# A hybrid decoder layer with 32 experts: what moves between HBM and SBUF per expert job, where a result row is stored, and which engines split the weights and combine the results

## The reference, cut to what matters

```python
top_v, top_e = lax.top_k(logits, TOP_K)          # TOP_K = 4, N_EXPERTS = 32
top_w = jax.nn.softmax(top_v, axis=-1)
...
def expert_block(args):                          # a block: up to 128 rows of one expert
    xb, e = args
    gu = xb @ w_gate_up[e] + b_gate_up[e]
    gate = jnp.minimum(gu[:, 0::2], SWIGLU_LIMIT)
    up = jnp.clip(gu[:, 1::2], -SWIGLU_LIMIT, SWIGLU_LIMIT)
    act = (up + 1.0) * gate * jax.nn.sigmoid(SWIGLU_ALPHA * gate)
    return act @ w_down[e] + b_down[e]
...
out = jnp.zeros((T, D)).at[row_tok].add(ys * row_w[:, None])
x = x + gate2 * out
```

## Time and profile before

| | |
|---|---|
| median of 3 executions | 2153.21 us (2151.19 to 2153.41) |
| the profiled execution's own time | 2149.9 us |
| its span | 2148.1 us |
| instructions | 28297 |
| busy: PE, DVE, ACT, POOL | 89%, 74%, 52%, 41% |
| bytes moved by DMA | 534.79 MB, 249 GB/s over the span |

### The profile page before, as it was taken

The page is one execution under the profiler, slowest core; times in us unless marked ns, Lnnn a source line. Parts: engine busy times, 40 slices in busy tenths (PEclk is TensorE's granted clock), DMA queues, the critical chain, the costliest instruction groups (busy, mean ns, idle before and its releaser), DMA issues.

```text
span 2148.1 us, 28297 instructions
## 1 busy us (share of the span) xinstructions
...
## 2 busy tenths in 40 slices
...
GB/s 349 292 63 0 313 2 2 1 141 1 2 48 148 79 52 128 350 353 351 350 360 347 352 348 354 359 345 354 355 351 360 348 353 357 347 354 346 351 363 231
DMA packets 249704, 534.79 MB, mean 249 GB/s; under 512 B 10635, under 2 KB 12744, under 8 KB 248436
## 3 DMA queue, kind: packets, MB, share of 16 engines
...
HBM read 495.76 MB, written 38.29 MB: 249 GB/s over the span
## 4 chain that ended last, share of the span: by engine, by line
PE 36%; DVE 11%; issue 11%; ACT 1%; DMA 1%; DVEq 1%; POOL 1%; POOLq 0%; ACTq 0%
PE bank L1815 11%; PE bank L1816 11%; PE bank L1814 11%; DVE sb_e_lo L1770 7%; PE bank L1811 2%; PE bank L1801 1%; PE bank L1829 1%; DVE sb_x_lo L2014 1%; DVE bank L2105 1%; DVE sb_mod L2024 1%; DVE sb_a_lo L2058 1%; ACT sb_x_hi L1894 0%; DMA sb_x_slot<-h_rows,sb_row_of 0%; DVE sb_bias_pick L2010 0%; POOL sb_e_lo L1770 0%
## 5 line engine op out<-in xcount | busy, mean ns | idle before, releaser
L1770 POOL TENSOR_TENSOR sb_e_lo<-sb_w_raw,sb_e_hi 128x512 fp32r<-128x512 f32 x388 | 673.9, 1746 | 496.7 <-ACT sb_e_hi L1891 377.4
L1770 DVE TENSOR_TENSOR sb_e_lo<-sb_w_raw,sb_e_hi 128x1536 fp32r<-128x1536 f32 x388 | 810.3, 2115 | 2.2 <-ACT sb_e_hi L1891 2.2
L1891 ACT CAST sb_e_hi<-sb_w_raw 128x2048 fp32r<-128x2048 f32 x389 | 741.4, 1906 | 99.0 <-PE bank L1816 48.5
L1814 PE MATMUL bank<-sb_e_hi,sb_x_hi 128*128 128x512 f32 x1032 | 415.2, 402 | 0.0
L1816 PE MATMUL bank<-sb_e_hi,sb_x_lo 128*128 128x512 f32 x1032 | 411.1, 398 | 0.0
L1815 PE MATMUL bank<-sb_e_lo,sb_x_hi 128*128 128x512 f32 x1032 | 411.1, 398 | 0.0
L1816 PEld LDWEIGHTS bank<-sb_e_hi,sb_x_lo 128*128 128x128 f32 x1032 | 197.8, 192 | 43.8
L2027 DVE SCALAR_TENSOR_TENSOR sb_mod<-sb_mod 128x256 f32<-128x256 f32 x129 | 223.6, 1734 | 4.5
L1815 PEld LDWEIGHTS bank<-sb_e_lo,sb_x_hi 128*128 128x128 f32 x1032 | 197.7, 192 | 41.3
L1814 PEld LDWEIGHTS bank<-sb_e_hi,sb_x_hi 128*128 128x128 f32 x1032 | 198.3, 192 | 37.8
L1814 PE MATMUL bank<-sb_e_hi,sb_a_hi 128*128 128x512 f32 x512 | 208.6, 407 | 7.6 <-POOL sb_e_lo L1770 7.6
(11 more groups left out here) (380 smaller groups left out, 2773.6 us busy)
## 6 DMA issues: line engine op xcount, KB each, us to landing
...
sb_w_raw<-in_w_down_dram SPq DMA_DIRECT2D x128, 1024.0 KB, 7.3
...
```

The costliest lines, as they stand in the source:

```text
L1770: return eng.tensor_tensor(g.e_lo[:, p % PARTS, rows, :], raw(p)[:, rows, :], g.e_hi[:, p % PARTS, rows, :].bitcast(F32), ALU.subtract)
L1814: te.matmul(out, hi[:, k0 + k, :], w_hi, start=(first and k == 0 and what >= 2 * GU), stop=False)
L1891: return sc.copy(g.e_hi[:, p % PARTS, :, :], raw(p))
```

## The change

- **Rows.** The routing table now carries goals: `goal_of` holds token * 4 + k for a used slot and 4096 (`EMPTY`) for an unused one, and `row_of` is that shifted right by 2. Gathers and stores are both indirect DMAs of POOL with a bounds check, so that unused slots move nothing. The store of `g.y` goes to row token * 4 + k of `y_rows`. DVE copies the job's column of `goal_of` to `goal_now` once the former store has landed (`y_out`), inside the loop after `row`. ACT no longer issues a store. The stores that filled the unused rows of `y_rows` in the RWKV phase are gone.
- **Split.** DVE takes all four rows of a piece (128x2048). POOL takes none; its turn is a one-element operation (`tick`), the store, another `tick`, and the gather.
- **First gather.** It is issued in the routing block, as soon as `row_of` is there; `x_slot` is zeroed before.
- **The end.** The four rows of a token now lie side by side, so SP reads them back with 8 plain DMAs of 1024 KB (128 tokens, two rows each). DVE builds 12 diagonal matrices of routing weights (`diag`, 128x128) at the end of routing; PE adds three of four rows of each token with them, 24 matmuls of 128x512 f32 behind the 8 of the bias; DVE adds the fourth out of PSUM into SBUF, and multiplies and adds as before, with one 128x1024 operation each.

```diff
+EMPTY = 2 * SEQ * TOP_K
 RING = 3
 MIN_JOBS, MAX_JOBS = SEQ * TOP_K // P, (SEQ * TOP_K + N_EXP * (P - 1)) // P
-SPARE = (MAX_JOBS + 1 - MIN_JOBS) // 4
...
-    step(pool.iota(g.token[:, :], [[P, NT]], base=0, channel_multiplier=1, allow_small_or_imprecise_dtypes=True))
+    step(pool.iota(g.goal[:, :, :], [[TOP_K * P, NT], [1, TOP_K]], base=-EMPTY, channel_multiplier=TOP_K, allow_small_or_imprecise_dtypes=True))
...
-        @block.sync
-        def _(sp):
-            for i in range(SPARE):
-                at = MIN_JOBS * P + 4 * P * i
-                sp.dma_start(g.y_rows[at:at + 4 * P, :].rearrange("(p r) n -> p (r n)", r=4), g.hT[:, :, :].rearrange("p k n -> p (k n)")).then_inc(g.y_spare, 16)
...
+PE_BACK = 3
...
+def gather_rows(g, po, at):
+    po.indirect_dma_start(out=g.x_slot[:, :], out_offset=None, in_=g.h2_rows[:, :], in_offset=bass.IndirectOffsetOnAxis(ap=at, axis=0),
+                          bounds_check=SEQ - 1, oob_is_err=False).then_inc(g.x_in, 16)
+def scatter_rows(g, po, sem):
+    po.indirect_dma_start(out=g.y_rows[:, :], out_offset=bass.IndirectOffsetOnAxis(ap=g.goal_now[:, 0:1], axis=0), in_=g.y[:, :], in_offset=None,
+                          bounds_check=SEQ * TOP_K + P - 1, oob_is_err=False).then_inc(sem, 16)
...
+            po.wait_ge(*pool.at("job_of"))
+            po.memset(g.x_slot[:, :], 0.0).then_inc(*pool("x_slot"))
+            po.wait_ge(*pool.at("x_slot"))
+            po.iota(g.goal_now[:, :], [[1, 1]], base=SEQ * TOP_K, channel_multiplier=1).then_inc(*pool("spare"))
+            po.wait_ge(*pool.at("spare"))
+            po.wait_ge(g.h2_out, 16 * NT)
+            po.wait_ge(*vec.at("tok"))
+            gather_rows(g, po, g.row_of[:, 0:1])
...
-            ve.tensor_scalar(g.place_i[:, :], g.place_i[:, :], P, None, ALU.add).then_inc(*vec("at"))
...
-            of_tile = lambda x: x.rearrange("p (t k) j -> p t (k j)", t=NT)
-            ve.tensor_tensor(of_tile(g.in_job[:, :, :]), of_tile(in_job), g.token[:, :].unsqueeze(2).broadcast_to([P, NT, TOP_K * JOBS]), ALU.mult).then_inc(*vec("in_tok"))
+            goal = g.goal[:, :, :].rearrange("p t k -> p (t k)")
+            ve.tensor_tensor(g.in_job[:, :, :], in_job, goal.unsqueeze(2).broadcast_to([P, units, JOBS]), ALU.mult).then_inc(*vec("in_tok"))
...
-            ve.tensor_copy(g.row_of[:, :], ps[0][:, 0:JOBS]).then_inc(*vec("tok"))
+            then(ve.tensor_scalar(g.goal_of[:, :], ps[0][:, 0:JOBS], float(EMPTY), None, ALU.add), "goal")
+            ve.tensor_scalar(g.row_of[:, :], g.goal_of[:, :], 2, None, ALU.logical_shift_right).then_inc(*vec("tok"))
...
+            for t in ts:
+                for k in range(PE_BACK):
+                    ve.tensor_scalar(g.diag[:, t, k, :], g.ident[:, :], g.prob[:, t, k:k + 1], None, ALU.mult).then_inc(*vec(f"d{t}{k}"))
...
-        def lo_part(eng, p, rows):
-            return eng.tensor_tensor(g.e_lo[:, p % PARTS, rows, :], raw(p)[:, rows, :], g.e_hi[:, p % PARTS, rows, :].bitcast(F32), ALU.subtract)
-        def back(u):
-            part = (g.e_hi, g.e_lo)[u // (2 * PARTS)][:, u // 2 % PARTS, :, :].rearrange("p k n -> p (k n)")
-            return part[:, D * (u % 2):D * (u % 2) + D].bitcast(F32)
+            return split_done[p % PARTS], 3 * turn + 1
+        def back(t, k):
+            part = (g.e_hi, g.e_lo)[t // 2][:, 2 * (t % 2) + k // 2, :, :].rearrange("p k n -> p (k n)")
+            return part[:, D * (k % 2):D * (k % 2) + D].bitcast(F32)
+        def back_pair(t, h):
+            return (g.e_hi, g.e_lo)[t // 2][:, 2 * (t % 2) + h, :, :].rearrange("p k n -> p (k n)").bitcast(F32)
...
+            sp.wait_ge(all_stored, 1)
+            by_token = g.y_rows[0:SEQ * TOP_K, :].rearrange("(t p k) n -> t p (k n)", p=P, k=TOP_K)
+            for t in ts:
+                for h in range(2):
+                    sp.dma_start(back_pair(t, h), by_token[t][:, 2 * D * h:2 * D * h + 2 * D]).then_inc(back_in[t][h], 16)
...
-            for i in range(8):
-                t, n = i // 2, i % 2
-                te.matmul(ps[i][:, :], g.wT[:, P * t:P * t + P], g.b_down[:, 512 * n:512 * n + 512], start=True, stop=True).then_inc(*last_pe(f"b{i}"))
+            for t in ts:
+                for n in range(2):
+                    te.matmul(ps[2 * t + n][:, :], g.wT[:, P * t:P * t + P], g.b_down[:, 512 * n:512 * n + 512], start=True, stop=False)
+            for t in ts:
+                for k in range(PE_BACK):
+                    if k % 2 == 0:
+                        te.wait_ge(back_in[t][k // 2], 16)
+                    for n in range(2):
+                        mm = te.matmul(ps[2 * t + n][:, :], g.diag[:, t, k, :], back(t, k)[:, 512 * n:512 * n + 512], start=False, stop=(k == PE_BACK - 1))
+                mm.then_inc(*last_pe(f"t{t}"))
...
-                sc.wait_ge(*act.at("y1", turn))
-                sc.dma_start(g.y_rows[bass.ds(turn * P, P), :], g.y[:, :]).then_inc(y_out, 16)
...
-            def gather_rows(at):
-                return po.indirect_dma_start(out=g.x_slot[:, :], out_offset=None, in_=g.h2_rows[:, :], in_offset=bass.IndirectOffsetOnAxis(ap=at, axis=0))
+            def tick(i):
+                po.tensor_tensor(g.tick[:, i:i + 1], g.ones[:, 0:1], g.ones[:, 0:1], ALU.mult).then_inc(ticked, 1)
             jobs = job_count(po)
-            gather_rows(g.row_of[:, 0:1]).then_inc(x_in, 16)
-            for i, p in enumerate(FIRST):
-                po.wait_ge(*first_act.at(f"g{i}"))
-                lo_part(po, p, slice(VEC_ROWS, 4)).then_inc(split_done[p % PARTS], 1)
             po.wait_ge(*first_pe.at("xt1"))
-            gather_rows(g.row_of[:, 1:2]).then_inc(x_in, 16)
-            for p in range(2):
-                po.wait_ge(*first_act.at(f"h{p}"))
-                lo_part(po, p, slice(VEC_ROWS, 4)).then_inc(split_done[p % PARTS], 1)
+            gather_rows(g, po, g.row_of[:, 1:2])
             with po.Fori(0, jobs) as turn:
-                for p in list(range(2, N_POS)) + [0, 1]:
-                    po.wait_ge(*(act.before("h2", turn) if p == 2 else act.at(f"h{p}", turn)))
-                    if p == 10:
-                        po.wait_ge(row_ready, turn + 1)
-                    lo_part(po, p, slice(VEC_ROWS, 4)).then_inc(split_done[p % PARTS], 1)
-                    if p == 10:
-                        gather_rows(g.row[:, 0:1]).then_inc(x_in, 16)
-            po.wait_ge(all_stored, 1)
-            for u in range(NT * TOP_K):
-                po.indirect_dma_start(out=back(u), out_offset=None, in_=g.y_rows[:, :],
-                                      in_offset=bass.IndirectOffsetOnAxis(ap=g.place_i[:, u:u + 1], axis=0)).then_inc(back_in[u], 16)
+                po.wait_ge(*act.at("y1", turn))
+                po.wait_ge(*vec.before("goal", turn))
+                po.wait_ge(ticked, 2 * turn + 1)
+                tick(0)
+                scatter_rows(g, po, y_out)
+                po.wait_ge(row_ready, turn + 1)
+                tick(1)
+                gather_rows(g, po, g.row[:, 0:1])
+            po.wait_ge(*last_act.at("y1"))
+            po.wait_ge(last_goal, 1)
+            scatter_rows(g, po, y_out)
...
-                return lo_part(ve, p, slice(0, VEC_ROWS)).then_inc(split_done[p % PARTS], 1)
+                return ve.tensor_tensor(g.e_lo[:, p % PARTS, :, :], raw(p), g.e_hi[:, p % PARTS, :, :].bitcast(F32), ALU.subtract).then_inc(split_done[p % PARTS], 1)
...
+                ve.wait_ge(y_out, 16 * turn + 16)
+                ve.tensor_scalar(g.goal_now[:, :], g.goal_of[:, bass.ds(turn, 1)], 0, None, ALU.add).then_inc(*vec("goal"))
...
+            ve.memset(g.unused[:, 1:2], 0.0).then_inc(last_goal, 1)
             ve.wait_ge(y_out, 16 * jobs + 16)
-            for p in range(2):
-                ve.wait_ge(*is_split(p, jobs))
             ve.memset(g.unused[:, 0:1], 0.0).then_inc(all_stored, 1)
             for t in ts:
-                ve.wait_ge(*last_pe.at(f"b{2 * t + 1}"))
-                sums = [ps[2 * t + n][:, :] for n in range(2)]
-                for k in range(TOP_K):
-                    u = TOP_K * t + k
-                    ve.wait_ge(back_in[u], 16)
-                    if k:
-                        ve.wait_ge(*last_vec.at(f"k{t}{k - 1}"))
+                ve.wait_ge(*last_pe.at(f"t{t}"))
+                for k in range(PE_BACK, TOP_K):
+                    if k == PE_BACK:
+                        ve.wait_ge(back_in[t][k // 2], 16)
                     for n in range(2):
-                        mm = ve.scalar_tensor_tensor(sums[n], back(u)[:, 512 * n:512 * n + 512], g.prob[:, t, k:k + 1], sums[n], ALU.mult, ALU.add)
-                    mm.then_inc(*last_vec(f"k{t}{k}"))
-                ve.wait_ge(*last_vec.at(f"k{t}{TOP_K - 1}"))
-                for n in range(2):
-                    mm = ve.tensor_tensor(g.mod[:, t % 3, 512 * n:512 * n + 512], sums[n], g.mod[:, 3, 512 * n:512 * n + 512], ALU.mult)
-                mm.then_inc(*last_vec(f"gate{t}"))
+                        at = slice(512 * n, 512 * n + 512)
```

(12 more changed lines are left out.)

41 lines of the change are left out of this document (20 added, 21 removed).

## The result

The changed kernel takes **2047.85 us**, median of 4 runs (2047.55 to 2048.57), against 2152.2 for the kernel before beside it: ratio 0.9521, 95% interval 0.9502 to 0.954. The profiled execution took 2048.57 with a span of 2046.5 (before: 2148.1), a gain of 101.6 us in span.

A forecast was written before the change was run, and what follows sets the result against it. PE, at 38.56 us a turn, was taken to wait for DVE's splits, which POOL's splits held up. Loop -83, start -5.5 and end -5 sum to -93.5: 2149.9 to 2056.4, plus 3.3 gives 2060 us, range 2044 to 2092.

The forecast's parts named there:

- Loop, -83: Job loop: with the split on DVE alone PE never waits and keeps its clock, 38.56 to 35.97 us a turn, 32 turns.
- the turn of 35.97: Job loop: PE's turn at full clock without its wait, 36.9 less 0.93 us, taken as the new turn.
- DVE's turn, 34.6 as an upper bound: Job loop: DVE's work a turn, 12 splits of 2.3 us plus 6.5 and 0.5, below PE's 35.97.
- Routing and first gather, -5.5: Ahead of the loop: earlier gather lets PE turn rows at 852.4, not 856.9 (-4.5), plus -1; bounds 0 and -8 us.
- 12 diagonals of 0.16 us delay the next block by 1.9 us, to 850.4: End of routing: DVE's diagonals set the next block's start; PE then does a 2 us bias product and turns rows at 852.4.
- -1: Start of the loop: 1 us gained because POOL's splits and second gather are no longer ahead of the first turn.
- The end, -5: After PE's last job matmul: store landing, reads, PE's products and last tile take 41.2 us against 46.3.
- Rows, 0: Job loop: moving only used rows earns nothing by itself, since a turn's transfers, 33.8 us at 388 GB/s, stay below PE.
- The store on POOL, 0: Job loop: the store lands some 10 us into a turn, DVE's wait comes at 24 to 25; 15 us of slack, price 0.
- The end at half clock: Rival, 0.13: the end's 24 PE products don't lift the clock, 48 passes take 41 us; 19 us worse, 2079.
- Slower by the new wait: Rival, 0.03: DVE's wait for the store's landing decides, from some 27 us into a turn; landing at 40 us costs +330.
- Bounds check saves nothing: Rival, 0.04: all 128 descriptors still move, 13.6 MB a turn takes 35.1 us, still hidden; 2062 us.

The follow-up runs named there:

- e1: Kernel before, with DVE splitting all four rows and a one-element POOL operation ahead of the gather; all rows still move, ACT still stores: 2056.5 us, ratio 0.9555.
- e2: Changed kernel with POOL's quarter of each split put back, DVE doing three quarters: 2165.67 us, ratio 1.0067 to the kernel before.
- e8: Changed kernel plus 12 two-input POOL subtractions of 128x512 a turn whose result nobody uses: 2284.46 us, ratio 1.0617 to the kernel before.
- e4: Changed kernel with the twelve diagonals built by ACT during routing, not by DVE: 2046.56 us, ratio 0.9511 to the kernel before.
- e11: Changed kernel with the routing block closed without GpSimd's drain: 2042.48 us, ratio 0.9495 to the kernel before.
- e5: Changed kernel with the down-bias products 128 rows high instead of 32, zeros below row 32: 2045.13 us, ratio 0.9489 to the kernel before.
- e9: Changed kernel plus, 12 times a turn on POOL, a one-element multiplication and a one-input 128x512 operation, both unused: 2279.8 us, ratio 1.0585 to the kernel before.

## Why the prediction was right, and where it was not

The direction, the mechanism and the range (2044 to 2092) hold; 2060 was 12 us too high. Of that, 8.1 is the sum (-93.5 forecast, -101.6 by span) and 3.8 the way from span to median: I added the 3.3 by which the median of before stood above its profiled execution, and the median after stands 0.7 below its own; 0.3 goes the other way, as this execution's own time is 2.1 above its span and the one of before 1.8. The last 0.3 is rounding.

- **Loop, -83: undersized by 11.8 us.** That DVE is freed from POOL, PE stops waiting and the clock stays at 1.00 is shown by e1, e2 and e8. The failed term is the turn of 35.97, which I took as 36.9 less the idle 0.93. That idle time counts from the modelled end of the overlapped matmul before. From start to start, the step into the waiting matmul is 1.31 us in place of 0.23, so the wait cost 1.08, and 1100.01 to 1136.87 without it is 35.78. Another 0.10 is the step behind that matmul, 0.33 (1100.01 to 1100.34) where it is 0.23 in the change. The last 0.08 to 35.60 was not traced.
- **DVE's turn, 34.6 as an upper bound:** busy 1047.90 / 32 = 32.7. The split was 2.28 (forecast 2.3), L2042 0.43 as forecast.
- **Routing and first gather, -5.5: -1.2 by stage, -2.2 counted from `row_of`.** The failed step is "12 diagonals of 0.16 us delay the next block by 1.9 us, to 850.4". The diagonals took 2.42 us, but the block came at 853.4, held by POOL's drain until the gather had landed, and not by DVE (e4, e11). With the drain gone, the rows come 9.2 us after `row_of` against 14.2 before: -5.0, where I had -4.5. The "-1" for POOL's splits ahead of the first turn is there in e1 (9.9 us from the rows to the loop, 11.0 before), but not in the change (11.1): eleven passes behind the rows ran at 0.63 us there, the lower clock, against six in e1. With the bias product at full height none did, and it was 9.4 (e5). The other 1.0 of the stage is that `row_of` itself came later in this execution.
- **The end, -5: -5.6.** The store had landed by 2010.47, 4.7 us after the last job matmul (forecast 5.1), and PE ended at 33.7 (34.2). The bias products were done 10.6 us after that matmul (12.0). Half clock reached into the first 24 of the 48 passes (12.8 us, the second 24 took 10.5): 2.4 us where I had 1.7.
- **Rows, 0:** e1 moves all rows and has the same turn within 0.06 us.
- **The store on POOL, 0:** issued at 905.4, landed 7.4 us later in the median, and DVE asked for it at 927.8: 15 us of slack, as forecast. But e2, with the store beside splits on POOL, is 0.7% dearer than the kernel before, a price that I had not put down. And `tick`, put at 0.1 us, takes POOL 2.13; POOL waits long before both, so it costs nothing here.

I cited the Trainium skill (DMA: Bandwidth & Descriptors, SWDGE vs HWDGE vs iDMA) for POOL's DMAs being held off by DVE. In the change the gather took POOL 2.67 us and the store 1.01, 2.35 in e2: held off in part, and never on the path. The store at 905.38, with DVE idle or on PSUM, took 1.02; the gather at 930.61, begun inside a split, took 2.92. That rule is about DVE's two-port modes, and no run here tells whether a split runs in one. The Trainium skill, SBUF — State Buffer (Who interferes with whom), says that a Vector instruction with two SBUF inputs contends with a GpSimd instruction that reads SBUF, and that one with at most one SBUF input, outside the two-port modes, does not. The rows agree: L2042 moves between 0.43, 1.11 and 1.18, L2074 stays at 0.42. By its words e9's POOL work, which reads SBUF, contends too; measured, DVE's split took 2.34 against 2.28 us, and the loser was POOL.

**The rivals.** The end at half clock came in part: 0.50 from 2012 to 2020 under a busy PE, then 1.00. It rose under the full-height products, as the Trainium skill (TensorE: Matmul & The Clock Gate, Part 1) has it of sustained matmul activity. Partly held: fell, no wait in the loop. Slower by the new wait: fell, 15 us of slack. Bounds check saves nothing: fell by the bytes, though every packet is still there.
